# A two-block transformer kernel: the product of probabilities and values taken once per head over all 512 queries, not twice per head over pairs of query tiles

## The reference, cut to what matters

```python
# block 1, "ml": 4 heads of 128, stabilised mLSTM (weights exp(d - m) times q k)
num = einsum('bhls,bhsv->bhlv', s, vc) + ...
# block 1, "mla": 4 heads, values of 128
pr = softmax(where(key_pos <= q_pos, s, -inf));   einsum('bhqk,bkhv->bqhv', pr, v)
# block 2, "df": 4 heads, two softmaxes per head
ad = pd[:, :, 0] - lam * pd[:, :, 1];             einsum('bhqk,bkhe->bqhe', ad, dv)
# block 2, "fx": 8 heads of 64, scores with a cumulative forget gate
pf = softmax(where(causal, sf, NEG));             einsum('bhqk,bkhd->bqhd', pf, fv)
```

## Time and profile before

| | us |
|---|---|
| median of 3 runs | 1390.58 |
| lowest, highest | 1388.3, 1391.17 |
| the profiled execution's own time | 1390.59 |
| its span, first to last instruction | 1388.8 |

### The profile page before, as it was taken

How to read it: one execution, slowest core, us unless ns; L and a number is a source line. 1 busy time by engine, 2 the same in 40 slices (tenths; PEclk the granted TensorE clock), 3 DMA queues, 4 the chain that set the end, 5 groups by cost and what they waited for, 6 DMA issues and landing times.

```text
span 1388.8 us, 17831 instructions
## 1 busy us (share of the span) xinstructions
PE 1319.3 (95%) x6548; PEld 1111.8 (80%) x6548; DVE 781.7 (56%) x1286; ACT 555.9 (40%) x914; POOL 44.9 (3%) x47
## 2 busy tenths in 40 slices
PE   7998878999999999999999999999899999999996
PEld 6877767789888888888777887877788788888886
DVE  5875667546644454323575787586685632355434
ACT  5645545444322323222454654465552322223221
POOL 3000000000000000000021000010000000000002
PEclk9998989999999999999999999999999999999998
DMA  5220110221223223333223332331211232223322
GB/s 176 92 91 16 47 38 31 92 76 61 91 92 98 98 91 106 120 101 101 92 90 117 92 99 84 88 91 35 92 62 61 91 106 91 91 92 104 106 91 76
DMA packets 37101, 120.46 MB, mean 87 GB/s; under 512 B 4508, under 2 KB 6556, under 8 KB 37040
## 3 DMA queue, kind: packets, MB, share of 16 engines
q1 hardware_dynamic: 36464, 117.98, 26.6%
q0 software_dynamic: 576, 1.65, 0.4%
HBM read 112.27 MB, written 2.11 MB: 82 GB/s over the span
## 4 chain that ended last, share of the span: by engine, by line
PE 81%; DVE 11%; ACT 4%; issue 2%; DMA 1%; POOL 0%; POOLq 0%; ACTq 0%; SPq 0%; DVEq 0%
PE bank L781 25%; PE bank L782 24%; PE bank L783 24%; DVE w_lo L1864 2%; DVE tiles L1864 2%; DVE tiles L1867 1%; DVE arena L1864 1%; PE bank L925 1%; ACT w_hi L1329 1%; PE bank L887 1%; PE bank L878 1%; DVE probsT L1864 1%; PE bank L946 1%; DVE arena L1867 1%; DMA raw_slab<-in_stream 1%
## 5 line engine op out<-in xcount | busy, mean ns | idle before, releaser
L1864 DVE TENSOR_TENSOR w_lo<-raw_slab,w_hi 128x1024 fp32r<-128x1024 f32 x199 | 244.4, 1228 | 297.9 <-ACT w_hi L1329 282.0
L781 PE MATMUL bank<-u_hi,w_hi 128*128 128x512 f32 x852 | 337.4, 396 | 14.5 <-DVE tiles L1864 3.4
L782 PE MATMUL bank<-u_lo,w_hi 128*128 128x512 f32 x852 | 334.1, 392 | 0.0
L783 PE MATMUL bank<-u_hi,w_lo 128*128 128x512 f32 x852 | 333.9, 392 | 0.0
L1329 ACT ACTIVATE w_hi<-raw_slab 128x1024 fp32r<-128x1024 f32 x189 | 199.1, 1054 | 184.7 <-PE bank L783 180.5
L781 PE MATMUL bank<-arena,w_hi 128*128 128x512 f32 (+1 forms) x672 | 254.0, 378 | 9.8 <-DVE w_lo L1864 4.9
L783 PE MATMUL bank<-arena,w_lo 128*128 128x512 f32 (+1 forms) x672 | 251.8, 375 | 0.0
L782 PE MATMUL bank<-arena,w_hi 128*128 128x512 f32 (+1 forms) x672 | 251.8, 375 | 0.0
L781 PEld LDWEIGHTS bank<-u_hi,w_hi 128*128 128x128 f32 x852 | 161.1, 189 | 50.9 <-DVE tiles L1864 4.0
L783 PEld LDWEIGHTS bank<-u_hi,w_lo 128*128 128x128 f32 x852 | 161.3, 189 | 34.3
L782 PEld LDWEIGHTS bank<-u_lo,w_hi 128*128 128x128 f32 x852 | 161.4, 189 | 31.7
(11 more groups left out here) (224 smaller groups left out, 1568.8 us busy)
## 6 DMA issues: line engine op xcount, KB each, us to landing
raw_slab<-in_stream SPq DMA_DIRECT2D x207, 512.0 KB, 3.4
arena<-arena SPq DMA_DIRECT2D x32, 128.0 KB, 2.3
residual<-in_xT SPq DMA_DIRECT2D x8, 256.0 KB, 8.1
out_hT<-residual SPq DMA_DIRECT2D x16, 128.0 KB, 1.7
arena<-forget_rows SPq DMA_DIRECT2D x8, 128.0 KB, 2.3
tiles<-in_pT POOLq DMA_DIRECT2D x2, 256.0 KB, 3.0
tiles<-bias_rows POOLq DMA_DIRECT2D x1, 512.0 KB, 4.1
tiles<-in_positions POOLq DMA_DIRECT2D x1, 256.0 KB, 3.4
```

Of the source, the lines that this page charges most:

```text
L781: pe.matmul(o, ws[0], xs[0], start=first, stop=False)
L782: pe.matmul(o, ws[0], xs[1], start=False, stop=False)
L783: return pe.matmul(o, ws[1], xs[0], start=False, stop=last)
L1864: return nc.vector.tensor_tensor(o, a, b, op)
```

## The change

Each head has one product with the values, at step 4 h + 8, when its last unit is in. For key tile j it takes the queries of tiles j to 3 at once: 512, 384, 256 and 128 columns, three matmuls each, 12 in all. `probsT` holds one head: for high and low 10 tiles of 128 columns, ordered by key tile, and each unit's columns are scattered into it. A unit of three or four key tiles is scattered by two copies on ScalarE and by two subtractions on VectorE, where there was one of each. `ctx_ready` counts heads: ScalarE's copy for unit n waits for n // 4 products. On VectorE, in each step, the scaling of unit s - 2 comes before the low half of unit s - 4, where it came after.

```diff
-PAIR_START, PAIR_COLS = (0, 3 * P), 11 * P
+KEY_START, HEAD_COLS = (0, 4 * P, 7 * P, 9 * P), 10 * P
...
-                use(("ctx", a, u // ST), CTX_BANKS[a][u // ST % len(CTX_BANKS[a])], (sem.ctx_ready, (UNIT0[a] + u + 1) // 2), free.get(a, (sem.mix_lo, n + 1)))
+                use(("ctx", a, u // ST), CTX_BANKS[a][u // ST % len(CTX_BANKS[a])], (sem.ctx_ready, (UNIT0[a] + u + 1) // ST), free.get(a, (sem.mix_lo, n + 1)))
...
-        def transposed(part, i):
-            start, n = PAIR_START[i // 2], i // 2 * 2 + 2
+        def transposed(part, i, o):
+            src_ = o[:, 0:(i + 1) * P].rearrange("p (j q) -> p j q", q=P)
             if i == 0:
-                return probsT[:, part, 0:P].rearrange("p (j q) -> p j q", q=P)
-            if i == 1:
-                return probsT[:, part, P:3 * P].rearrange("p (j q) -> p j q", q=P)
-            return probsT[:, part, start:start + n * 2 * P].rearrange("p (j q) -> p j q", q=2 * P)[:, 0:i + 1, i % 2 * P:(i % 2 + 1) * P]
+                return [(probsT[:, part, 0:P].rearrange("p (j q) -> p j q", q=P), src_)]
+            pieces = [(probsT[:, part, i * P:(i + 6) * P].rearrange("p (j q) -> p j q", q=3 * P)[:, :, 0:P], src_[:, 0:2])]
+            if i == 2:
+                pieces.append((probsT[:, part, 7 * P:8 * P].rearrange("p (j q) -> p j q", q=P), src_[:, 2:3]))
+            elif i == 3:
+                pieces.append((probsT[:, part, 8 * P:10 * P].rearrange("p (j q) -> p j q", q=P), src_[:, 2:4]))
+            return pieces
...
+            def head_values(a, h, last_unit, values):
+                b, before, _ = uses[("ctx", a, h)]
+                if before:
+                    pe.wait_ge(*before)
+                pe.wait_ge(sem.pT_lo, last_unit + 1)
+                o = bank[b]
+                def moved(j):
+                    return [probsT[:, part, KEY_START[j]:KEY_START[j] + (ST - j) * P] for part in range(2)]
+                w, x = values(h, 0), moved(0)
+                pe.matmul(o[:, :], w[0], x[0], start=True, stop=False)
+                for j in range(1, ST):
+                    three(o[:, j * P:S], values(h, j), moved(j), False, False)
+                pe.matmul(o[:, :], w[0], x[1], start=False, stop=False)
+                pe.matmul(o[:, :], w[1], x[0], start=False, stop=True).then_inc(sem.ctx_ready, 1)
...
-                    if 0 <= v < units and v % 2:
...
+                    if 0 <= v < units and v % ST == ST - 1:
+                        head_values(a, v // ST, UNIT0[a] + v, values)
...
-                        if n >= 4:
-                            act.wait_ge(sem.ctx_ready, n // 2 - 1)
-                        nc.scalar.activation(transposed(0, v % ST), by_key_tile(o, w), ACT.Copy).then_inc(sem.pT_hi, 1)
+                        if n >= ST:
+                            act.wait_ge(sem.ctx_ready, n // ST)
+                        for dst, part_ in transposed(0, v % ST, o):
+                            last = nc.scalar.activation(dst, part_, ACT.Copy)
+                        last.then_inc(sem.pT_hi, 1)
...
+                    normalise(step, units)
                     v = step - LAG_LO
                     if 0 <= v < units:
                         n = UNIT0[a] + v
-                        w = (v % ST + 1) * P
                         dve.wait_ge(sem.pT_hi, n + 1)
-                        low(transposed(1, v % ST), by_key_tile(bank[uses[("pT", a, v)][0]], w),
-                            transposed(0, v % ST)).then_inc(sem.pT_lo, 1)
-                    normalise(step, units)
+                        o = bank[uses[("pT", a, v)][0]]
+                        for (dst, part_), (hi, _) in zip(transposed(1, v % ST, o), transposed(0, v % ST, o)):
+                            last = low(dst, part_, hi)
+                        last.then_inc(sem.pT_lo, 1)
...
-            dve.wait_ge(sem.ctx_ready, UNIT0["fx"] // 2)
+            dve.wait_ge(sem.ctx_ready, UNIT0["fx"] // ST)
```

More of the change, by code:

```diff
@@ L536, in build @@
         forget_rows = nc.alloc_sbuf_tensor_at("forget_rows", [P, S], F32R, offset=tiles_at + -tiles_at % 32 + SSUM * S * 4)
-        probsT = sb("probsT", [P, 2, PAIR_COLS], F32R)
+        probsT = sb("probsT", [P, 2, HEAD_COLS], F32R)
         raw = sb("raw_slab", [P, 2, SLAB * P], F32)
@@ L589, in bias_tile @@
             return flat[:, at_:at_ + BIAS_W]
-        def transposed(part, i):
-            start, n = PAIR_START[i // 2], i // 2 * 2 + 2
+        def transposed(part, i, o):
+            src_ = o[:, 0:(i + 1) * P].rearrange("p (j q) -> p j q", q=P)
             if i == 0:
-                return probsT[:, part, 0:P].rearrange("p (j q) -> p j q", q=P)
-            if i == 1:
-                return probsT[:, part, P:3 * P].rearrange("p (j q) -> p j q", q=P)
-            return probsT[:, part, start:start + n * 2 * P].rearrange("p (j q) -> p j q", q=2 * P)[:, 0:i + 1, i % 2 * P:(i % 2 + 1) * P]
-        def by_key_tile(o, w):
-            return o[:, 0:w].rearrange("p (j q) -> p j q", q=P)
+                return [(probsT[:, part, 0:P].rearrange("p (j q) -> p j q", q=P), src_)]
[5 more added lines that the diff above has]
+            return pieces
         def prob_slot(a, v):
@@ L929, in attention @@
                     v = step - LAG_PV
-                    if 0 <= v < units and v % 2:
[L931 to L942, removed]
-                                three(alone, w, x, False, False)
-                            else:
-                                x = [probsT[:, part, c:c + 2 * P] for part in range(2)]
-                                pe.matmul(both, w[0], x[0], start=j == 0, stop=False)
-                            if j == 0:
-                                first_w, first_x = w, x
-                                continue
-                            if j < i:
-                                pe.matmul(both, w[0], x[1], start=False, stop=False)
-                                pe.matmul(both, w[1], x[0], start=False, stop=False)
-                        pe.matmul(both, first_w[0], first_x[1], start=False, stop=False)
-                        last = pe.matmul(both, first_w[1], first_x[0], start=False, stop=True)
-                        last.then_inc(sem.ctx_ready, 1)
+                    if 0 <= v < units and v % ST == ST - 1:
+                        head_values(a, v // ST, UNIT0[a] + v, values)
                     if tail and at_head(a, step, LAG_HEAD + 1) is not None:
```

## The result

The changed kernel takes 1425.13 us (median of 4 runs, 1424.03 to 1425.62) against 1390.62 us for the kernel before: ratio 1.025, 95% interval 1.0233 to 1.0268, or 34.5 us more. The forecast was 1406.4, its range 1392 to 1418. The direction was right; the size was less than half of what came.

What follows compares the result with a forecast made beforehand. TensorE's own work was taken as the bound, 81% of the chain of waits. To 1390.59 us the attentions added +2, +7.0, -1 and +8.3 and the small edits -0.5, together +15.8: 1406.4 us, range 1392 to 1418.

Steps and rivals of the forecast that it cites:

- The third attention: Third attention: a 2.75 us projection behind the product hides the new wait; -1 us, bounds -1.6 and +3.
- The relief: Third attention: TensorE gains 0.4 us four times from the shorter product, against a stall of 0.25 three times.
- idle in the third attention: Sign that the prediction is wrong; it expected no new idle time of TensorE in the third attention.
- The fourth attention: Fourth attention: eight heads, seven waits of ScalarE for a product; +8.3 us, bounds +3 and +12.
- the meeting: Once per head ScalarE's copy waits for the product, VectorE for the copy, TensorE for VectorE; 0.9 us idle if uncovered.
- The second attention: Second attention: no projections cover the wait, a head takes 9.25 us in place of 7.08; +7.0 us, bounds +3.5 and +13.
- The first attention: First attention: three waits for a product, partly slack since VectorE already waits there; +2 us, bounds 0 and +6.
- The clock rival: Second attention: TensorE's granted clock falls; +6 to +14 us more, 1412 to 1420; chance 0.12.
- The product: All four attentions: 12 matmuls for 18 per head, 1.93 us for 2.32; about 0.4 us less per head.
- the rival on weight loads: TensorE's products: each of 120 removed matmuls frees a 0.204 us load, 24 us for 8; 1390; chance 0.06 with no change.
- VectorE's order: VectorE scales before the low half and may start 0.2 to 0.4 us sooner; -0.5 us, bounds 0 and -3.
- The scatter: Units 2 and 3: 40 more instructions each on ScalarE and VectorE, at most 6.4 us per engine; 0.1 each counted.

Runs made afterwards that it cites:

- taken_first: Changed kernel, but VectorE takes a finished projection out of its bank before it waits for the low half: 1422.3 us, ratio 1.0238.
- product_first: Changed kernel with the product at the start of TensorE's step, ahead of that step's transposes and scores: 1410.0 us, ratio 1.015.
- second_rows: Changed kernel, but in the second and fourth attention odd heads keep key rows 0 and 1 in four other tiles: 1410.3 us, ratio 1.0165.
- split_product: As second_rows, with the product there cut in two, between transposes and scores and behind the scores: 1409.8 us, ratio 1.0145.
- wait_only: Kernel before with the changed kernel's wait and VectorE's new order, products and buffer still by pairs: 1406.3 us, ratio 1.0118.
- two_pieces: As wait_only, with copies and low halves of units 2 and 3 in two pieces each: 1412.7 us, ratio 1.0164.
- swap_only: Kernel before with only VectorE's order changed, scaling ahead of the low half: 1387.1 us, ratio 0.9986.
- swap_again: The same kernel as swap_only, run a second time: 1387.6 us, ratio 0.9994.

## Why the prediction was wrong

- **The third attention (forecast -1, bounds -1.6 and +3; measured +7.7): the step that failed.** "Behind the product stands a fill of 2.75 us in the same step, which hides the copy, the low half and the two exponentials behind them." The fill was free of ScalarE's copy, but not of VectorE: its bank was to be freed by an instruction queued behind the waiting low half. The prediction saw VectorE's "projection and slab work" shift by 4 us but had TensorE come for it only at E + 6.85 (E is the end of the product), a stall of 0.25; the fill right behind the product needs it at E. Measured were 1.35, 1.35 and 1.34 us there, and 0.82, 1.44 and 0.35 two steps later. taken_first, which only moves that work ahead, has no stall behind the product. The relief booked against it (0.4 us four times) did not come either: TensorE's busy time in this attention is 74.93 us, not less than the 73.85 before. The prediction itself had named "idle in the third attention" as a sign of being wrong. 100% busy was read as cover; it meant that every stall is lost in full.
- **The fourth attention (+8.3; measured +13.4).** From product end to product end the increments are 0.5, 2.0, 4.4, 0.5, 1.3, 0.5, 2.5 and 1.7 us; the sum had 0.5, 0.5, 2.6, 0.5, 1.1, 0.5, 1.7 and 1.0. TensorE idles behind the product at steps 12, 20, 28 and 32 and not at 8, 16 and 24, as forecast. But the way on from step 8, where a projection hides the meeting itself, cost 2.0 and not 0.5 (the stall of 1.41 below comes later), and the dear ones were sized by the first stall alone. Of the 4.4 us 1.1 is the clock: that product takes 3.06 us, not 1.97 (965.36 to 968.42). The changed kernel's timeline, in the fourth attention, shows the stall repeating before it ends:
```profile
948.13 0.33 PE L943 MATMUL bank<-square,tiles 128*128 128x128 f32 x1 [1.41 <-DVE probsT L1859]
...
955.03 0.55 PE L943 MATMUL bank<-square,tiles 128*128 128x128 f32 x3 [0.75 <-DVE probsT L1859]
...
959.40 0.65 PE L943 MATMUL bank<-square,tiles 128*128 128x128 f32 x4 [0.73 <-DVE probsT L1859]
...
962.76 0.33 PE L943 MATMUL bank<-square,tiles 128*128 128x128 f32 x1 [2.29 <-DVE probsT L1859]
```
- **The second attention (+7.0; measured +7.6).** The meeting is as forecast (idle 0.75). The size is partly luck: from product end to product end the two middle periods are 8.90 and 8.22 us where they were 7.07 and 6.41, 1.8 us more each where 2.15 was booked; the first product came 2.0 us late where 0.45 was booked (2.23 us idle at 236.78, for a low half); the last period grew by 2.0 (2.3). The errors cancel.
- **The first attention (+2, bounds 0 and +6; measured +5.3 in the profiled run).** It is about +1 (taken_first +0.8, product_first +1.1, second_rows +1.2) with a granted clock of 0.86 to 0.89, and mostly more where the clock is lower: changed kernel 0.81, split_product (+7.5) 0.79.
- **The clock rival** named the second attention and was given 0.12. Part of it came, mostly in the first attention: 0.81 for 64.39 us in place of 0.88 for 59.12 is 24.5 against 14.2 us at 1.2 GHz ((1 - clock) x 2 x length), up to 5 us more if TensorE is the bound. The same working gives up to 2 us each in the second (0.96 to 0.92) and the fourth (1.00 to 0.98): up to 9 of the 34 us. The rival had the size about right and the place wrong. It runs through the repeats too: taken_first ran at 1415.3 us with a mean clock of 0.979 and at 1422 to 1423 with 0.972.
- **The product (gain 0.4 us a head; measured 0.2).** 12 matmuls take 1.97 us to the start of the projection behind them (936.24 to 938.21), near the forecast 1.93. Before, a pair's 6 take 0.69 where the next matmul follows at once, not the 0.87 of the earlier trace rows, as the kernel before shows in its third attention:
```profile
815.72 0.28 PE L946 MATMUL bank<-probsT,arena 128*128 128x256 f32 x1
...
816.41 0.40 PE L781 MATMUL bank<-u_hi,w_hi 128*128 128x512 f32 x1
```
  With 1.45 for the other pair, six matmuls fewer save 1.45 + 0.69 - 1.97 = 0.17 us. That also refutes the rival on weight loads: at 0.204 us a load they would have saved 1.2. The Trainium skill, "TensorE: Matmul & The Clock Gate" (Part 3, The mechanism), lets loads overlap only when the row group differs; this measurement goes against it. The same page, Part 2 (Step-by-step), also allows it for a load that targets the background weight buffer, and with that the 0.17 us agrees (no trace here shows which buffer a load goes to).
- **VectorE's order (-0.5, bounds 0 and -3).** It measured -2.2 and -2.0 us, within the bounds, and not to be told from nothing.
- **The scatter** was counted at 0.1 us a piece inside the sums. On wait_only its 80 pieces cost 5.4 us, each against its own kernel before; TensorE's idle time in the second to fourth attention grew by 1.4 of it, and most of the rest goes with a lower clock.

By kernels, each against its own kernel before: the wait makes 17.0 us (wait_only), the pieces 5.4 more (two_pieces), and the change from two products per head to one late one the remaining 12.1. In idle time of TensorE, second to fourth attention, the three steps are 12.5, 1.4 and 9.8 us. These do not add strictly, since each changes what is late next. The first step is shown by a kernel that holds nothing else but VectorE's order. The last is explained only in part: product_first, which ends the product earlier, took back 15 us, but the part of the later end and that of the missing early product are not separated. Open is also how much the clock has in each, and whether the change causes the lower clock.

## What to carry to other kernels

Before cover is booked against a new wait, follow each operand of the covering instruction, its output bank too, back to the queue position of what frees it: if that stands behind the wait, there is no cover. Fewer and longer instructions on the bound engine are worth their count (0.2 us a head here); one buffer less of slack between three engines cost a round trip per reuse (0.75 us idle here) and further stalls behind it. If such a wait must be, put its releaser first in its step, so that the engine's other work covers the round trip; where nobody waits for it, leave it late. Before two profiles are compared, compare their granted clock and the idle time, not the length alone.

## What the runs showed of the hardware

The half-speed clock comes and goes between executions of one kernel: swap_only and swap_again are the same program, and their profiles have 87.54 us at a granted clock of 0.96 and 84.63 at 1.00 for the fourth attention; the ten executions of swap_only run from 1383.8 us (mean clock 0.984) to 1394.1 (0.976). It does so in the first attention too, where all engines wait for each other: with the same instructions there, second_rows had 60.34 us at 0.89, the changed kernel 64.39 at 0.81 and split_product 66.60 at 0.79. A difference of some 6 us in one profile of this kernel is therefore no evidence by itself; nor is the length of the stretch that an edit touches, unless its granted clock is the same.
